# Rows of an expert layer: dots and sums of one ring of gathers laid out as one sequence, with eleven places late and five sums inside the routing steps

## What is computed

```python
def _peer_block(hb, ib, gb, down, up):
    u = down[ib]
    pre = jnp.einsum('td,thkd->thk', hb, u).astype(jnp.float32)
    w = (gb * jax.nn.gelu(pre, approximate=False)).astype(hb.dtype)
    return jnp.einsum('thk,thkd->td', w, up[ib])
...
        x = x + gate_f * peer(h2, ...)
    return rms_norm(x, final_norm_gain)
```

## Time and profile before

| | |
|---|---|
| median of three runs | 1702.98 us |
| the profiled execution | 1706.08 us |
| its span | 1704.1 us |
| TensorE busy | 1598.3 us (94%) |
| VectorE busy | 1250.8 us (73%) |
| ScalarE busy | 552.2 us (32%) |
| POOL busy | 661.1 us (39%) |
| moved by DMA | 499.16 MB, mean 293 GB/s |
| the chain that ended last | DMA 34%, VectorE 26%, TensorE 25%, POOL 5% |

### The profile page before, as it was taken

One profiled execution on the slowest core, in us unless ns is written; L12 is line 12 of the kernel. 1 busy time (PEld: TensorE's weight loads), 2 busy tenths in 40 slices (PEclk: granted clock), 3 DMA queues, 4 the chain that ended last, 5 costly groups with the idle time before them and its releaser, 6 DMA issues.

```text
span 1704.1 us, 20375 instructions
## 1 busy us (share of the span) xinstructions
PE 1598.3 (94%) x6936; PEld 1169.8 (69%) x6936; DVE 1250.8 (73%) x2390; ACT 552.2 (32%) x1355; POOL 661.1 (39%) x590
## 2 busy tenths in 40 slices
PE   4998999998998999999999999998999998999973
PEld 2886877776886998888888889887444443444431
DVE  6866456778465679999987889989666665676677
ACT  3432244454622632111227788776000000000000
POOL 0000111110002415434765667656644544455464
PEclk8999999999999999999999999999999999999997
DMA  8424422234422437999999999999999999999997
GB/s 338 180 93 147 153 81 80 63 122 152 179 102 78 182 124 275 404 377 383 387 403 368 374 387 391 382 371 362 402 409 409 409 410 412 409 409 410 409 404 286
DMA packets 126278, 499.16 MB, mean 293 GB/s; under 512 B 15456, under 2 KB 15840, under 8 KB 115808
## 3 DMA queue, kind: packets, MB, share of 16 engines
q0 software_dynamic: 75776, 269.52, 40.7%
q1 hardware_dynamic: 50400, 228.35, 35.0%
HBM read 492.04 MB, written 4.72 MB: 292 GB/s over the span
## 4 chain that ended last, share of the span: by engine, by line
DMA 34%; DVE 26%; PE 25%; POOL 5%; issue 4%; ACT 4%; DVEq 3%; SPq 0%; ACTq 0%
DMA ring<-in_up,idx 24%; DMA ring<-in_down,idx 9%; DVE ring L1613 7%; PE bank L566 6%; PE bank L567 5%; PE bank L568 5%; POOL ring L1867 5%; PE bank L855 4%; DVE accum L1856 3%; DVE acc_ada L1247 2%; PE bank L842 1%; ACT whi L891 1%; DVE wlo L1272 1%; DVEq L1281 1%; DVE att_max L1427 1%
## 5 line engine op out<-in xcount | busy, mean ns | idle before, releaser
L868 PE MATMUL bank<-stream,wmat 128*128 128x512 f32 x1024 | 443.8, 596 | 10.9 <-DMA stream<-in_up 7.0
L855 PE MATMUL bank<-h2T,stream 128*128 128x256 f32 x2048 | 452.8, 379 | 0.0
L1856 DVE SCALAR_TENSOR_TENSOR accum<-ring,share,accum 128x1024 f32<-128x1024 f32 x245 | 314.7, 1284 | 174.3 <-DMA ring<-in_up,idx 171.4
L1867 POOL DMA_INDIRECT ring<-in_down,idx x256 | 323.1, 1262 | 254.9 <-DVE pre L1613 173.6
L855 PEld LDWEIGHTS bank<-h2T,stream 128*128 128x128 f32 x2048 | 384.2, 190 | 49.5
L868 PEld LDWEIGHTS bank<-stream,wmat 128*128 128x128 f32 x1024 | 195.8, 191 | 258.3 <-issue 246.4
L1867 POOL DMA_INDIRECT ring<-in_up,idx x256 | 263.8, 1030 | 239.5 <-DVE accum L1856 211.2
L1613 DVE CUSTOM_DVE_ANT_0 ring<-ring,h2row 128x1024 f32<-128x1024 f32 x256 | 306.9, 1219 | 40.9 <-DMA ring<-in_down,idx 38.2
L566 PE MATMUL bank<-hT_hi,whi 128*128 128x512 f32 (+1 forms) x504 | 189.8, 377 | 11.8 <-DVE hT_lo L1314 9.5
L568 PE MATMUL bank<-hT_hi,wlo 128*128 128x512 f32 (+1 forms) x504 | 184.9, 367 | 0.0
L567 PE MATMUL bank<-hT_lo,whi 128*128 128x512 f32 (+1 forms) x504 | 184.6, 366 | 0.0
(11 more groups left out here) (230 smaller groups left out, 1830.7 us busy)
## 6 DMA issues: line engine op xcount, KB each, us to landing
stream<-in_downT SPq DMA_DIRECT2D x128, 512.0 KB, 6.8
stream<-in_up SPq DMA_DIRECT2D x128, 512.0 KB, 6.8
raw<-in_ada SPq DMA_DIRECT2D x16, 1024.0 KB, 4.9
raw<-in_w_query SPq DMA_DIRECT2D x16, 1024.0 KB, 4.9
ada_raw<-in_ada SPq DMA_DIRECT2D x8, 1024.0 KB, 16.3
raw<-in_w_xp SPq DMA_DIRECT2D x4, 1024.0 KB, 12.5
raw<-in_w_gateA SPq DMA_DIRECT2D x4, 1024.0 KB, 4.8
raw<-in_w_branchP SPq DMA_DIRECT2D x4, 1024.0 KB, 4.9
```

What stands on the lines that cost most here:

```text
L855: last = pe.matmul(bank[:, 4 + i % 2, 0:DT], stream[:, i % RING, k * P:(k + 1) * P], h2T[:, k, GB * P:S], start=(k == 0), stop=(k == KT - 1))
L868: last = pe.matmul(bank[:, 2 * tb + half, :], wmat[:, i, tb * P:(tb + 1) * P], stream[:, (ET + i) % RING, half * S:(half + 1) * S], start= ...
L1856: dve.scalar_tensor_tensor(accum[:, b, :], ring[slot][:, :], share[:, b, k:k + 1], accum[:, b, :], ALU.mult, ALU.add).then_inc(sum_done, 1)
L1867: pool.indirect_dma_start(out=ring[slot][:, :], out_offset=None, in_=table, in_offset=bass.IndirectOffsetOnAxis(ap=idx[:, b, k:k + 1], axi ...
```

## The change

Dots and sums are one sequence of 512 rows, t = 0 to 255 dots and 256 to 511 sums, with one table for their places (`place_rows`); `rows_done(n)` does the next n, dot or sum. In the routing steps a third row now comes at every third step (MORE_DOTS = 3), so that 261 rows are done with the last step: 256 dots and five sums. Gelu of block 0 stands in ScalarE's step 84, and the product into `share` stands before the first sum of each block; that first sum writes `accum` instead of adding to it, and the clearing is gone. `accum` lies on `h2row`'s memory (140 KB), and its old memory (196 KB) gives two more places, 11 and 12. From row 266 on the places are eleven, six of which open behind the routing products. Nine sums and not eleven are TensorE's, and the output blocks 2 and 3 are made six sums later.

```diff
-URING = 9
+LATE_SLOTS = (0, 1, 2, 3, 4, 5, 6, 7, 8, 11, 12)
+BEHIND_ROUTING = (4, 5, 6, 7, 11, 12)
+GELU_AT = 84
...
-MORE_DOTS = 4
+MORE_DOTS = 3
...
-LATE_DOTS = 256
+LATE_ROWS = 261
...
-SUM_PE = tuple(range(219, 252, 3))
+SUM_PE = tuple(range(225, 252, 3))
...
-Y_AT = {150: 0, 222: 2, 229: 3}
+Y_AT = {150: 0, 228: 2, 235: 3}
...
-        accum = place("accum", [P, GB, D], f32, 196)
+        accum = place("accum", [P, GB, D], f32, 140)
...
+        def place_rows():
+
+            late = LATE_ROWS + len(STEP_SLOTS)
+            for t in range(2 * GB * P):
+                slots = EARLY_SLOTS if t < EARLY_DOTS else STEP_SLOTS if t < late else LATE_SLOTS
                 slot = min(slots, key=lambda n: at_slot[n][-1] if at_slot[n] else -1)
...
+                if i == GELU_AT:
+                    gelu_dots(0)
...
+            def add(g):
+
+                b, k = g // P, g % P
+                if k == 0:
+                    dve.wait_ge(gel_ready, b + 1)
+                    dve.tensor_tensor(share[:, b, :], share[:, b, :], pre[:, b, :], ALU.mult)
+                    dve.drain()
+                    dve.sem_inc(share_ready, 1)
+                row = row_arrived(dve, GB * P + g)
+                if k == 0:
+                    last = dve.tensor_scalar(accum[:, b, :], row[:, :], share[:, b, k:k + 1], None, ALU.mult)
+                else:
+                    last = dve.scalar_tensor_tensor(accum[:, b, :], row[:, :], share[:, b, k:k + 1], accum[:, b, :],
+                                                    ALU.mult, ALU.add)
+                last.then_inc(sum_done, 1)
+                dve.drain()
...
-                dots(STEP_DOTS + (i % MORE_DOTS == 0 and len(quads_at(i)) == 1))
-            assert done[0] == LATE_DOTS, done
+                rows_done(STEP_DOTS + (i % MORE_DOTS == 0 and len(quads_at(i)) == 1))
+            assert done[0] == LATE_ROWS, done
             dve.drain()
             dve.sem_inc(w_ready, 1)
-            dots(P, P)
-            dve.drain()
-            dve.sem_inc(pre_ready, 1)
-
-            dve.memset(accum[:, :, :], 0.0)
...
+            for t in range(2 * GB * P):
+                g = t % (GB * P)
+                b, k, prior = g // P, g % P, row_prior[t]
...
+                if prior is None and row_slot[t] in BEHIND_ROUTING:
                     pool.wait_ge(gmm, DT // 4)
+                elif prior is not None and prior < GB * P:
+                    pool.wait_ge(dot_done, prior + 1)
+                elif prior is not None:
+                    who, n = summed(prior - GB * P)
+                    pool.wait_ge(pe_summed if who == "pe" else sum_done, n)
+                gather(down if t < GB * P else up, b, k, row_slot[t])
```

More of the change, by code:

```diff
@@ L480, in layer, with row_arrived @@
         N_MEAN = dict(norm1=0, norm2=1)
-        down_slot, down_round, down_prior = [], [], []
+        row_slot, row_round, row_prior = [], [], []
         at_slot = [[] for _ in ring]
[L485 to L489, removed]
+        def place_rows():
+            late = LATE_ROWS + len(STEP_SLOTS)
+            for t in range(2 * GB * P):
+                slots = EARLY_SLOTS if t < EARLY_DOTS else STEP_SLOTS if t < late else LATE_SLOTS
                 slot = min(slots, key=lambda n: at_slot[n][-1] if at_slot[n] else -1)
[L491 to L496, removed]
+                row_prior.append(at_slot[slot][-1] if at_slot[slot] else None)
+                row_slot.append(slot)
+                row_round.append(len(at_slot[slot]) + 1)
+                at_slot[slot].append(t)
+        def row_arrived(eng, t):
+            eng.wait_ge(ring_in[row_slot[t]], 16 * row_round[t])
+            return ring[row_slot[t]]
+        place_rows()
         def w_done(eng, n):
@@ L874, in _ @@
             for n, g in enumerate(SUM_PE):
-                slot = g % URING
                 pe.wait_ge(diag_ready, n + 1)
-                pe.wait_ge(ring_in[slot], 16 * (len(at_slot[slot]) + g // URING + 1))
+                row = row_arrived(pe, GB * P + g)
                 for half in range(2):
-                    last = pe.matmul(bank[:, 4 + half, :], diag[:, n % 2, :], ring[slot][:, half * S:(half + 1) * S],
+                    last = pe.matmul(bank[:, 4 + half, :], diag[:, n % 2, :], row[:, half * S:(half + 1) * S],
                                      start=(n == 0), stop=(n == len(SUM_PE) - 1))
@@ L1152, in exponentials, with gelu_dots @@
                 act.activation(dst, dst, ACT.Exp).then_inc(exp_done, 1)
+            def gelu_dots(b):
+                act.wait_ge(pre_ready, b + 1)
+                act.activation(pre[:, b, :], pre[:, b, :], ACT.Gelu).then_inc(gel_ready, 1)
             def pick_out(b):
@@ L1208, in _ @@
                     copy_rest(q, i)
-            for b in range(GB):
-                act.wait_ge(pre_ready, b + 1)
-                act.activation(pre[:, b, :], pre[:, b, :], ACT.Gelu).then_inc(gel_ready, 1)
+            gelu_dots(1)
             def square(tb, n):
@@ L1606, in _, with dot, rows_done @@
             done = [0]
[L1608 to L1616, removed]
+            def dot(g):
+                b, k = g // P, g % P
+                row = row_arrived(dve, g)
+                dve.tensor_tensor_reduce(out=row[:, :], in0=row[:, :], in1=h2row[:, b, :], scale=1.0, scalar=0.0,
+                                         op0=ALU.mult, op1=ALU.add, accum_out=pre[:, b, k:k + 1]).then_inc(dot_done, 1)
+                if k == P - 1:
+                    dve.drain()
+                    dve.sem_inc(pre_ready, 1)
+            def add(g):
+                b, k = g // P, g % P
+                if k == 0:
[10 more added lines that the diff above has]
+                last.then_inc(sum_done, 1)
+                dve.drain()
+            def rows_done(count):
+                for t in range(done[0], done[0] + count):
+                    if t < GB * P:
+                        dot(t)
+                    else:
+                        add(t - GB * P)
+                    done[0] = t + 1
             credit = [FIRST_CREDIT]
@@ L1623, in fill @@
                     credit[0] -= ROUTE_PER_DOT
-                    dots(1)
+                    rows_done(1)
             def top16(vals, at_, src, fill):
@@ L1760, in _ @@
             dve.sem_inc(routes_done, 1)
-            dots(DOTS_EXP)
+            rows_done(DOTS_EXP)
             for b in range(DB):
@@ L1765, in _ @@
                 softmax(b)
-            dots(DOTS_PICK)
+            rows_done(DOTS_PICK)
             def one_hots(q):
@@ L1840, in scale_out @@
                                          gain_row[:, :], ALU.mult, ALU.mult).then_inc(out_ready, 1)
-            for g in range(GB * P):
-                b, k, slot = g // P, g % P, g % URING
+            rows_done(max(0, GB * P - done[0]))
+            for g in range(done[0] - GB * P, GB * P):
                 if g in Y_AT:
@@ L1852, in _ @@
                     dve.drain()
[L1853 to L1858, removed]
+                if g not in SUM_PE:
+                    add(g)
             y_make(1)
@@ L1906, in _ @@
                 wlo_make(n)
-            for g in range(GB * P):
-                b, k = g // P, g % P
-                if k == 0:
+            for t in range(2 * GB * P):
+                g = t % (GB * P)
+                b, k, prior = g // P, g % P, row_prior[t]
+                if t < GB * P and k == 0:
                     pool.wait_ge(idx_ready, b + 1)
-                if g == 0:
+                if t == 0:
                     pool.wait_ge(x1_stored, 16)
-                if down_prior[g] is not None:
-                    pool.wait_ge(dot_done, down_prior[g] + 1)
-                elif RING <= down_slot[g] < 8:
+                if prior is None and row_slot[t] in BEHIND_ROUTING:
                     pool.wait_ge(gmm, DT // 4)
[L1917 to L1921, removed]
-                    pool.wait_ge(pe_summed if who == "pe" else sum_done, n)
[L1923 to L1927, removed]
+                elif prior is not None and prior < GB * P:
+                    pool.wait_ge(dot_done, prior + 1)
+                elif prior is not None:
+                    who, n = summed(prior - GB * P)
+                    pool.wait_ge(pe_summed if who == "pe" else sum_done, n)
+                gather(down if t < GB * P else up, b, k, row_slot[t])
 def constants():
```

16 lines of the change are left out of this document (4 added, 12 removed).

## The result

The changed kernel takes 1709.66 us, the median of 20 runs (1703.41 to 1714.01), against 1705.05 for the kernel before, also of 20 (1699.26 to 1711.13). The ratio is 1.0031, with a 95% interval of 1.0019 to 1.0042: about 5 us slower, where 3.5 us faster was forecast, and outside the range. The profiled execution of the change took 1707.51 us, its span 1705.5 us. A trace is one execution, and the times of a kernel scatter by some 6 us either side of its median.

The account below looks back on a forecast made before the run. The prediction took DMA bytes at 410 GB/s to set the end. Its terms, +6.3 - 7.7 - 1.6 - 0.5 = -3.5 us, gave a median of 1699.5 us, range 1693.5 to 1706.5.

Parts of the forecast that it names:

- What bounds the kernel: From 1215 us on, DMA bytes at a flat 410 GB/s set the end, with TensorE beside them; a row costs 1.28 us.
- The lead: At the start of the second pass over `up`, 6 rows more already moved: -7.7 us (-7.0 to -8.3).
- part (1): Routing steps: five rows more cost 4 us (0 to 8.0) plus 2.3 in the last steps; second pass 6.3 later.
- The gap (3): Behind the routing steps: no clearing, early Gelu and unbroken sums recover lost DMA time, -1.6 us (0 to -2.1).
- signs named ahead: Changed profile: second pass near 1196, steps about 380 GB/s, no 5 us below 300 behind them, stream ending near 1647.
- The bound of 1208: Start of the second pass: the forecast was to be wrong if it came past 1208 us.
- the ring is the whole limit: Rival, routing steps: each row costs its 2.0 us, +0.5 in all, so 1703.5 us; chance 0.15.
- Swallowed: Rival, routing steps: VectorE's idle time takes the four rows, start slips 2.3 only, -7.5, so 1695.5 us; chance 0.20.
- The lighter steps no longer make good: Rival, routing steps: VectorE stays behind after three-row steps, from 2.05 us a row; +9.4 to +25.7 us; chance 0.06.
- The plateau lifted: Rival, second pass and tail: eleven places raise 410 GB/s to 426, 18 us more saved, so 1681.5 us; chance 0.06.
- (4): Eleven places for nine: nothing in the second pass, -0.5 us in the tail (0 to -1.5).
- (5): Output sums: TensorE's go from 11 to 9, output rows 2 and 3 six sums later; no cost while the lead holds.

## Why the prediction was wrong

**What bounds the kernel** held: the end follows the bytes, 410 GB/s is a cap, and TensorE's second pass lies beside them. The lead, worked out as six rows at 1.28 us, with the gap's and the tail's share, came to -9.8 us, and the tail is 9.8 us shorter. That the two agree so closely is in part luck, since the gap's share in it did not come (below).

**The step that failed is part (1)**, "in such stretches they are free; in the others each costs what the ring takes, 2.0. Bounds 0 and 8.0 us. I take 4". The four rows cost 9.0 us, and the last steps' sums 4.3 and not 2.3. I took 1.85 us a row, the best 35 rows, for a pace that the ring can hold. It cannot: over the whole stretch it is about 2.0 at five places, whatever is asked (the table). Over 35 rows in a row the pace ranges from 1.85 to 2.10 in the kernel before, and from 1.90 to 2.08 in the change; the 1.85 was the best draw from this scatter. It follows directly on the longest wait for a landing, so some of it may be the ring catching up:

```profile
985.66 1.23 DVE L1613 CUSTOM_DVE_ANT_0 ring<-ring,h2row 128x1024 f32<-128x1024 f32 x1 [2.43 <-DMA ring<-in_down,idx]
```

The catching up could be 2.4 us of the 5 us by which the 35 rows beat a pace of 2.0; where the rest comes from stays open. The upper bound was too low as well, by 1.0 us, which is within the scatter of that stretch, and by 2 us since I bounded the last steps by VectorE's work alone: the fifth sum waited 2.08 us for its row.

With 13.3 us for the 6.3 of the forecast, the sum is 13.3 - 7.7 - 1.6 - 0.5 = +3.5, against +5.0, and 1.4 of the rest is the second pass's scatter in this pair of traces. The sum comes this near with a -1.6 in it that the next paragraph takes away, so it proves less than it seems to.

**The gap (3)** did not go as forecast, though the total hides it. The first 20 us behind the last routing product moved 294, 329, 348 and 321 GB/s, which is 4.2 us lost at 410; before, the windows from 1185 on moved 304, 256, 389 and 415, 3.4 us lost. So this term was not -1.6 but about +0.8. The first and the last of them, of the kernel before:

```profile
1185.00:1190.00 5.00, 1.14 (x10) 0.94 (x9) 4.69 (x10) 0.57 (x3) 3.79 (x3) 1.00 0.89 304
...
1200.00:1205.00 5.00, 5.00 (x13) 2.19 (x12) 2.81 (x3) 0.00 (x0) 4.08 (x4) 1.00 1.03 415
```

The clearing is gone, but POOL, behind five sums in order, is late with the places that open there: it issued the gather into the first of them 10.6 us behind the last routing product, 7.3 us before the change. So the lead, or the tail, must have given some 2 us more than I gave them; which of the two stays open.

Of the signs named ahead, the second pass started at 1199.55 and not near 1196, the steps moved 376 GB/s and not 380 or more, one window behind them fell to 294, and the stream ended at 1651.9 and not at 1647, with 23 gathers issued behind it (25 forecast). The bound of 1208, past which the forecast was to be wrong, was too loose: the time had left the range well before it.

**Rival "the ring is the whole limit"** (0.15) was the right mechanism, priced at +0.5 by a slip of 10.3 where 13.3 was measured. *Swallowed* is what happens with six places, not with five. *The lighter steps no longer make good* did not come: the pace stayed at 2.02, under the 2.05 from which it was to decide, and VectorE's work was not the reason for the waits (half the bytes, 273.94 us). *The plateau lifted* did not come either (nine places, no difference). The ceiling of 435 GB/s that the Trainium skill gives (DMA: Bandwidth & Descriptors, Specifications) was reached in no stretch shown here; the highest of the 40 slices of any run is 412. Eleven places at no gain in the second pass (4) held. Nine sums by TensorE at no cost (5) was tested by no run of its own.

## What to carry to other kernels

A ring's rate is its places divided by the time of one turn, and a local stretch that is faster than the mean is not a pace that it can hold. Work moved from a late stage into an earlier one pays only if the earlier one has the missing resource: here 8% of the DMA rate was free there (376 of 410 GB/s), but places were not, so a row cost 1.65 to 2.0 us to bring 1.28. Find the buffer first (here one place that the stream can spare while its steps are slow), and then the same move gains.

## What the runs showed of the hardware

TensorE stood idle for 8.19 us ahead of the second pass, and the granted clock was 0.53 in the 5 us up to 1200 and 0.50, the level of 1.2 GHz, from 1200 to 1205, against 0.66 for 5 us after the 3.87 us of the kernel before. No cost of it shows: the second pass took 450.2 to 452.5 us in all the traces, and the one of 452.3 with 251 rows had only 4.64 us of idle ahead of it.

The first sum of a block, one tensor times a scalar per partition, took 0.75 us for 128 x 1024, against 1.28 for the sum with an accumulator; I had priced both alike.

A turn of a place grew with the number of places, 9.2 us with four, 9.9 with five, 11.2 with six at the highest demand run with each, while the rate rose from 329 to 371 to 398 GB/s. A further place is worth less than its share already well below the 410 at which it is worth nothing.
